# Rotary swap by on-chip transfers, and a turn of the identity ahead of rows of products

## What is computed

```
z = x @ w_in                       # u, v, q, k, val, gates side by side
q = rope(q.reshape(b, 256, 8 heads, 2, 64), cos, sin)
k = rope(k.reshape(b, 256, 8 heads, 2, 64), cos, sin)

def rope(x, cos, sin):             # the rotary embedding
    x1, x2 = split(x, 2, axis=-1)  # 32 values each
    return concatenate([x1 * cos - x2 * sin, x2 * cos + x1 * sin], axis=-1)

h_a = gelu(u) * sgu(layernorm(gelu(v)))   # "sgu": 128x128 products per group
o   = differential attention of q, k, val
m   = sigmoid(g1) * (h_a @ w_branch[0]) + sigmoid(g2) * (rmsnorm(o) @ w_branch[1])
out = m @ w_out
```

## Time and profile before

| | |
|---|---|
| median of 3 runs | 1830.66 us (1828.44 to 1833.03) |
| the profiled execution | 1825.48 us |
| its span in the profile | 1823.6 us |
| granted TensorE clock, mean | 0.995 |
| TensorE busy | 1789.7 us (98%) |
| DVE, ACT, POOL busy | 1136.4, 867.9, 247.0 us |
| DMA, mean | 181 GB/s, 53.2% of the 16 engines on SP's queue |

### The profile page before, as it was taken

The page is one execution under the profiler, slowest core; times in us unless marked ns, Lnnn a source line. Parts: engine busy times, 40 slices in busy tenths (PEclk is TensorE's granted clock), DMA queues, the critical chain, the costliest instruction groups (busy, mean ns, idle before and its releaser), DMA issues.

```text
span 1823.6 us, 31041 instructions
## 1 busy us (share of the span) xinstructions
PE 1789.7 (98%) x12819; PEld 1617.9 (89%) x12819; DVE 1136.4 (62%) x1735; ACT 867.9 (48%) x1412; POOL 247.0 (14%) x264
## 2 busy tenths in 40 slices
PE   9999999999999999999999999999999999999999
PEld 8998699999899879996899997999776877879999
DVE  5754587676766466655675876566655655565553
ACT  5454344664444435443535753545345355445543
POOL 2000232121200020001231212000111443100000
PEclk9999999999999999999999999999999999999999
DMA  8665654545666666754755455775443433346663
GB/s 285 195 219 192 233 186 159 165 139 191 206 208 209 204 208 231 231 185 161 250 169 185 135 168 193 234 242 182 165 152 93 110 98 93 117 159 190 203 194 111
DMA packets 252396, 330.56 MB, mean 181 GB/s; under 512 B 13162, under 2 KB 213072, under 8 KB 252256
## 3 DMA queue, kind: packets, MB, share of 16 engines
q1 hardware_dynamic: 248240, 315.31, 53.2%
q0 software_dynamic: 4016, 13.27, 2.1%
HBM read 327.51 MB, written 1.05 MB: 180 GB/s over the span
## 4 chain that ended last, share of the span: by engine, by line
PE 64%; issue 24%; DVE 6%; POOL 2%; ACT 2%; DMA 1%; POOLq 0%; DVEq 0%; ACTq 0%
PE bank L714 14%; PE bank L717 14%; PE bank L715 14%; PE bank L737 5%; PE bank L739 5%; PE bank L740 5%; DVE X L1930 1%; DVE wlo L1852 1%; ACT whi L1402 1%; PE bank L1250 1%; PE bank L1272 1%; POOL rs L2447 1%; DMA G<-in_lam_dram 1%; PE bank L898 1%; PE bank L936 1%
## 5 line engine op out<-in xcount | busy, mean ns | idle before, releaser
L1852 DVE TENSOR_TENSOR wlo<-raw,whi 128x1024 fp32r<-128x1024 f32 x537 | 663.8, 1241 | 374.6 <-ACT whi L1402 370.5
L1402 ACT ACTIVATE whi<-raw 128x1024 fp32r<-128x1024 f32 x549 | 574.4, 1052 | 393.6 <-PE bank L740 171.7
L714 PE MATMUL bank<-XTh,whi 128*128 128x256 f32 x1984 | 560.7, 283 | 0.0
L717 PE MATMUL bank<-XTh,wlo 128*128 128x256 f32 x1984 | 551.8, 278 | 2.9 <-DVE wlo L1852 2.9
L715 PE MATMUL bank<-XTl,whi 128*128 128x256 f32 x1984 | 551.6, 278 | 0.0
L717 PEld LDWEIGHTS bank<-XTh,wlo 128*128 128x128 f32 x1984 | 372.9, 188 | 3.3 <-DVE wlo L1852 3.3
L715 PEld LDWEIGHTS bank<-XTl,whi 128*128 128x128 f32 x1984 | 374.8, 189 | 1.0
L714 PEld LDWEIGHTS bank<-XTh,whi 128*128 128x128 f32 x1984 | 372.9, 188 | 2.9
L714 PE MATMUL bank<-HCh,whi 128*128 128x256 f32 (+1 forms) x880 | 252.5, 287 | 0.9 <-DVE tmp L2343 0.9
L717 PE MATMUL bank<-HCh,wlo 128*128 128x256 f32 (+1 forms) x880 | 248.1, 282 | 0.0
L715 PE MATMUL bank<-HCl,whi 128*128 128x256 f32 (+1 forms) x880 | 248.1, 282 | 0.0
(11 more groups left out here) (342 smaller groups left out, 2419.6 us busy)
## 6 DMA issues: line engine op xcount, KB each, us to landing
raw<-in_ffn_w_dram SPq DMA_DIRECT2D x131, 1024.0 KB, 5.1
raw<-in_w_in_dram SPq DMA_DIRECT2D x76, 1024.0 KB, 5.0
raw<-in_w_mod_dram SPq DMA_DIRECT2D x24, 1024.0 KB, 5.0
raw<-in_w_branch_dram SPq DMA_DIRECT2D x16, 1024.0 KB, 5.0
raw<-in_w_out_dram SPq DMA_DIRECT2D x12, 1024.0 KB, 4.9
raw<-in_w_ffn_gate_dram SPq DMA_DIRECT2D x11, 1024.0 KB, 5.1
raw<-in_w_ffn_up_dram SPq DMA_DIRECT2D x11, 1024.0 KB, 5.1
raw<-in_w_ffn_down_dram SPq DMA_DIRECT2D x8, 1024.0 KB, 5.1
```

The costliest lines, as they stand in the source:

```text
L714: e.matmul(o, hi[:, k, w0:w0 + nc_], xh, start=first and k == 0, stop=False)
L717: m = e.matmul(o, lo[:, k, w0:w0 + nc_], xh, start=False, stop=last and k == nk - 1)
L1402: e.activation(hi_part(n), raw_part(n), ACTF.Copy).then_inc(WHI.did(n), 1)
L1852: e.tensor_tensor(lo_part(n), raw_part(n), hi_part(n).bitcast(F32), ALU.subtract).then_inc(WLO.did(n), 1)
```

## The change

**Rotation.** `rotate` and `perm` leave TensorE. After its copy of qk n into `s`, ACT waits for that copy's own semaphore and starts four transfers of 32 partitions by 256 values (32 KB each) from `s` to `u`, each to the partitions of the other block; one of four new semaphores `ROT` counts them. DVE multiplies `s` with cos one round after the copy, and `u` with sin (in place, now from SBUF) two rounds after it. POOL adds two rounds after. The ring `mtmp` has six buffers, and `u` n needs the sum of n - 3 to be through. `settle` makes one transpose of the identity into an unused part of a bank: ahead of the 16 products qk, and at the end of `modulation`, of which it takes over the semaphore. The table of constants loses 128 columns. The pieces below are, in this order: TensorE (three), ACT (`turned` and its rounds), DVE, POOL.

```diff
+            def settle(b):
+                return e.transpose(bank[b][:, 256:384], ident, ident)
...
-                        mm = e.matmul(bank[b][:, 2 * j:2 * j + 2], SUMS[i][m][:, j * 128:(j + 1) * 128], sel[:, at:at + 2],
-                                      start=m == 0, stop=m == 1)
-                mm.then_inc(MOD.did(("columns", g)), 1)
+                        e.matmul(bank[b][:, 2 * j:2 * j + 2], SUMS[i][m][:, j * 128:(j + 1) * 128], sel[:, at:at + 2],
+                                 start=m == 0, stop=m == 1)
+                settle(b).then_inc(MOD.did(("columns", g)), 1)
...
-                def rotate(n):
-                    b = 4 + n % 2
-                    q.wait_ge(AMX, ("qk", l, n))
-                    empty(b)
-                    e.matmul(bank[b][:, 0:T], perm, mtmp[tm[l].slot["s", n]][:, :], start=True, stop=True).then_inc(
-                        SMALL.did(("perm", l, n)), 1)
-                    emptied[b] = ((DMX, ("sin", l, n)),)
+                empty(3)
+                settle(3)
                 for n in range(16):
...
                     emptied[b] = ((AMX, ("qk", l, n)),)
-                    if n:
-                        rotate(n - 1)
...
+                def turned(n):
+                    ring_free(q, tm[l], ("u", n))
+                    q.wait_ge(AMX, ("qk", l, n))
+                    for p in range(0, 128, 32):
+                        e.dma_start(mtmp[tm[l].slot["u", n]][p:p + 32, :], mtmp[tm[l].slot["s", n]][p ^ 32:(p ^ 32) + 32, :]).then_inc(
+                            ROT[n % 4].did(("turned", l, n), by=16), 16)
+
                 for n in range(16):
                     w.pass_by(1)
                     q.wait_ge(MM, ("qk", l, n))
                     ring_free(q, tm[l], ("s", n))
                     e.activation(mtmp[tm[l].slot["s", n]][:, :], bank[n % 4][:, 0:T], ACTF.Copy).then_inc(AMX.did(("qk", l, n)), 1)
+                    turned(n)
...
                 for n in range(16):
                     w.pass_by(1)
                     if n:
-                        rotate(n - 1)
+                        times_cos(n - 1)
+                    if n > 1:
+                        times_sin(n - 2)
+                times_cos(15)
...
                 for n in range(16):
                     w.pass_by(1)
-                    if n:
-                        rotate(n - 1)
+                    if n > 1:
+                        rotate(n - 2)
```

More of the change, by code:

```diff
@@ L32 @@
 C_ID, C_SHARED, C_CM = 0, 128, 128
-C_COS, C_SIN, C_PERM, C_FIRST = 384, 640, 896, 1024
+C_COS, C_SIN, C_FIRST = 384, 640, 896
 C_COSG, C_SING, C_PERMG, C_SCAN, C_GM, C_IN, C_NEG, C_CMB, C_ALL = (
-    1024, 1280, 1536, 1664, 2432, 2688, 2944, 3200, 3202)
+    896, 1152, 1408, 1536, 2304, 2560, 2816, 3072, 3074)
 R_GB, R_DG, R_C, R_CC, R_N1, R_N2, R_BM, R_BA, R_GN, R_NQ, R_NK, R_ALL = (
@@ L393, in program @@
         BIAS = [signal(f"s_bias{h}") for h in range(8)]
+        ROT = [signal(f"s_rotary{i}") for i in range(4)]
         MM, TURN, SMALL, MOD = [signal("s_pe_" + n) for n in ("gemm", "turn", "small", "mod")]
@@ L437, in program @@
         sb(xst, "gap1", [128, 68])
-        cm, cos, sin, perm = csa[:, 0:256], csa[:, 256:512], csa[:, 512:768], csa[:, 768:896]
+        cm, cos, sin = csa[:, 0:256], csa[:, 256:512], csa[:, 512:768]
         def ffn_bufs(st, name, at=STANDS):
@@ L453, in program @@
             G = sb(st, "G", [128, 16, T])
-            mtmp = some(st, "mtmp", 4, [128, T])
+            mtmp = some(st, "mtmp", 6, [128, T])
             sm = sb(st, "sm", [128, 16])
@@ L547, in program @@
         for l in range(2):
-            r = Ring(4)
+            r = Ring(6)
             for n in range(16):
-                r.use(("s", n), (SMALL, ("perm", l, n)), (DMX, ("cos", l, n)))
-                if n:
-                    r.use(("u", n - 1), (PMX, ("rot", l, n - 1)))
+                r.use(("s", n), (ROT[n % 4], ("turned", l, n)), (DMX, ("cos", l, n)))
+                r.use(("u", n), (PMX, ("rot", l, n)))
             for n in range(8):
                 r.use(("g", n), (XLO, ("ha", l, n)))
-                if n == 0:
-                    r.use(("u", 15), (PMX, ("rot", l, 15)))
             for n in range(8):
@@ L1956, in mixer, with times_cos, times_sin @@
                     e.scalar_tensor_tensor(V[:, t, :], V[:, t, :], rs[:, t, 1:2], gb[:, 1, :], ALU.mult, ALU.add).then_inc(DMX.did(("v", l, t)), 1)
[L1958 to L1963, removed]
+                def times_cos(n):
+                    dst, j, scale = (Q, K)[n // 8], n % 8, (0.125, 1.0)[n // 8]
+                    q.wait_ge(AMX, ("qk", l, n))
                     e.scalar_tensor_tensor(dst[:, j, :], mtmp[tm[l].slot["s", n]][:, :], scale, cos, ALU.mult, ALU.mult).then_inc(
                         DMX.did(("cos", l, n)), 1)
+                def times_sin(n):
+                    u, scale = mtmp[tm[l].slot["u", n]], (0.125, 1.0)[n // 8]
+                    q.wait_ge(ROT[n % 4], ("turned", l, n))
+                    e.scalar_tensor_tensor(u[:, :], u[:, :], scale, sin, ALU.mult, ALU.mult).then_inc(DMX.did(("sin", l, n)), 1)
                 for n in range(16):
@@ L1983, in mixer @@
                     w.pass_by(1)
-                    if n == 0:
-                        rotate(15)
-                    else:
+                    if n < 2:
+                        times_sin(14 + n)
+                    if n:
                         low("ha", HAl, HAh, n - 1, mtmp[tm[l].slot["g", n - 1]])
@@ L2470, in rotate @@
                     dst, j = (Q, K)[n // 8], n % 8
+                    q.wait_ge(DMX, ("sin", l, n))
                     q.wait_ge(DMX, ("cos", l, n))
@@ L2483, in mixer @@
                     e.tensor_tensor(s[:, :], s[:, :], SG[:, n, :], ALU.mult).then_inc(PMX.did(("a", l, n)), 1)
-                    if n == 0:
-                        rotate(15)
+                    if n < 2:
+                        rotate(14 + n)
                 w.pass_b(8, 2)
```

6 lines of the change are left out of this document (1 added, 5 removed).

## The result

| | before | changed |
|---|---|---|
| median | 1829.76 us (1828.44 to 1833.03) | 1850.85 us (1848.42 to 1857.08) |
| ratio, 95% interval | 1 | 1.0118 [1.0086, 1.0149] |
| profiled execution, its span | 1825.48, 1823.6 us | 1848.42, 1846.7 us |
| the interval in layer 1 from the first qk product to val | 79.4 us | 92.6 us |
| TensorE busy | 98% | 96% |

The change makes the kernel 1.2% slower; the forecast was 1814.6 us. The mixers of the two layers lose 13.2 and 13.0 us, and the turns after `modulation` win some of it back.

A forecast was written before the change was run, and what follows sets the result against it. TensorE, busy 98%, was taken to bound the kernel, with ACT slowest in the changed qk rounds. 1825.48 - 5.3 (turns) - 10.8 (both mixers) + 5.2 (profiled execution to median) gave 1814.6 us, range 1807 to 1834.

The forecast's parts named there:

- Part 1, the turn: After `modulation`, one turn at five seams brings 1344 products from 117.8 to 113.3 ns: net 5.3 us won.
- Rival B: The turn doesn't set the pace or sets it to 118 ns; loss of 0.6 us there, 1820.5 us; chance 0.13.
- Part 2, what leaves TensorE: In the mixer, rotation products and waits go; TensorE alone would reach val 8.6 us earlier a layer.
- I take 0.42 for a start: One transfer start on ACT takes 0.42 us, four 1.68, so ACT's qk round is 3.17 us.
- rival C: Starts on ACT cost as much as L652's: 1833.6 us at 0.64, 1850 at 0.8; chance of above 0.58: 0.20.
- The sum 1.49 + 4d for ACT's round: ACT's qk round is its other work, 1.49 us, plus four transfer starts of d us each.
- first sign of being wrong: The forecast is wrong if a transfer start takes over 0.47 us or under 0.37.
- In sgu and the u rounds ACT catches up, having no transfers there: After qk 15 ends at 280.1, sgu adds 3.8 us and u 21.8, val at 305.7: 5.4 us earlier a layer.
- Part 3, the cover: Landing is hidden twice over, POOL's later sums take 0.74 us, weight chunks lose little with DMA at 0.59.
- The stop at round 3 for POOL's sum 0: ACT's round 3 starts wait for POOL's sum, 1.65 us beside busy DVE, until 248.3; then 3.17 us a round.
- Sum: Profiled 1825.48 less 5.3 for turns and 10.8 for both mixers, plus 5.2 to the median: 1814.6 us.

The follow-up runs named there:

- swap_no_turn: The changed kernel without any turn (transpose of the identity), rotation by transfers kept: 1856.3 us, ratio 1.0153 to the kernel before.
- mod_turn: The kernel before with only one transpose of the identity after each group of two-column products in `modulation`: 1818.4 us, ratio 0.9952.
- best_no_turn: The changed kernel with two starts each on ACT and SP, sgu adds ahead of DVE's round 14, eight ring buffers, no turns: 1819.9 us, ratio 0.9947.
- no_transfers: The changed kernel without any transfer of the swap; the product with sin reads the copy of qk itself: 1805.3 us, ratio 0.9862.
- split_sg13: The changed kernel with two starts on ACT and two on SP, and DVE's sgu adds ahead of round 14: 1808.6 us, ratio 0.9898.
- eight_starts: The changed kernel with each transfer cut in two, eight starts of 16 KB a round on ACT: 1927.9 us, one execution.
- sg13: The changed kernel with DVE's eight sgu adds moved ahead of its weight part of round 14, four starts still on ACT: 1829.9 us, ratio 1.0010.
- two_starts: The changed kernel with two transfers of 64 KB on ACT instead of four, leaving out the swap of blocks of 32: 1816.8 us, ratio 0.9928.
- split_starts: The changed kernel with two of each swap's four transfers started by SP instead of ACT: 1824.3 us, ratio 0.9967.
- sg_early: The changed kernel with DVE's eight sgu adds in round 14, one weight part later than ahead of that round: 1834.8 us, ratio 1.0034.

## Why the prediction was wrong

**Part 1, the turn:** right. The five seams run at 113 ns. As a size, 5.3 us agrees with one pair of runs (5.5 to 6.4, changed and swap_no_turn) and lies below two (8.8 with mod_turn, about 13 with best_no_turn); what those have beyond it isn't explained. Rival B is refuted. The Trainium skill, "TensorE: Matmul & The Clock Gate", section "Back-to-back issue gap", gives one distance for a number of columns, and gives it for the isolated product; the traces don't agree with it for a stream of them: both paces stand in every trace here, and a turn moves products from one to the other.

**Part 2, what leaves TensorE:** right in sum, 8.6 us a layer foretold and 8.4 with no_transfers, with two sizes off that cancel. The first four rounds ran at 118 ns and not at 113, and so TensorE stood 1.03 us at qk 4 instead of 1.6. In layer 1 of split_sg13 they ran at 113, and it stood 1.43: the low part sets when qk 4 goes on.

**Part 3, "I take 0.42 for a start":** wrong size. It was 0.61 (2.44 for four). "SP's number there barely depends on size" held. The forecast took weight chunks (one start of 1 MB and then another) for the nearest rows; the rows of L652, which it put into rival C, were nearer. The sum 1.49 + 4d for ACT's round held: 3.93 by it with 0.61, 3.91 in the trace, and with 8d within 0.1 in eight_starts (6.37 and 6.46). A start over 0.47 was the forecast's own first sign of being wrong. The Trainium skill, "DMA: Bandwidth & Descriptors", section "Issuing engines are not separate DMA queues", calls the time to initiate a transfer usually small relative to the transfer. A single start agrees, 0.61 against a landing of 2.5 us, but with four of them they are the largest part of ACT's round.

**"In sgu and the u rounds ACT catches up, having no transfers there":** this step failed, and it is the larger part of the error. The forecast followed ACT's lag only to TensorE's next weight part. It didn't follow it to DVE, whose adds for sgu stand behind DVE's waits for ACT. With rival C's formula at d = 0.61, which has no such coupling, val begins at 248.3 + 12 x 3.93 + 2.44 + 2.1 + 13.6 = 313.6, for a qk start at 231.67. sg13, which takes away only that coupling, has its qk start at 230.04 and val at 312.1: by the formula 312.0. So close an agreement is in part luck: the starts of round 3 came at 245.85 in sg13, where the shifted formula has 246.67, and the twelve rounds behind took 3.99 us in the mean and not 3.93. The changed kernel has 324.5. So from 305.7 (forecast) to 324.5 are 7.9 us by the size of a start and about 10.9 by the missing step: 10.3 of it sgu itself, and of these 1.6 the clock after the wait. The stages say the same: qk ends at 288.4 instead of 280.1, and sgu takes 10.3 us more than the 3.8 foretold. Rival C had the size of a start, but at d = 0.61 it gives 1825.48 + 5.1 - 5.3 + 5.2 = 1830.5 us, 20 below the result: the same step was missing in it. That is about what sg13 measured without the coupling (1829.9, ratio 1.0010). C's 1850 us for d = 0.8 is near the result for another reason, as no start was that long in the mean.

**Part 3, the cover:** landing (2.5 us), POOL's sum (0.74) and DMA share (0.59) bind nothing, as foretold. The stop at round 3 for POOL's sum 0, from which the forecast counts, hardly came in the changed kernel (0.05 us in layer 1, about 0.4 in layer 2), as the sum took 0.73 us and not 1.65 and ACT was late already. It came, with 3.7 us, in the kernels with two starts on ACT.

**Sum.** The mixers were to win 10.8 us and lost 26.2. With the 5.3 of the turns that is +20.9 us; the medians differ by 21.1, the profiled executions by 22.9.

## What to carry to other kernels

A transfer start is an instruction of its engine with a price of its own, per start and not per byte: multiply it by the starts a round, add it to that engine's other work, and compare the sum with the round of the bounding engine before moving anything there, an engine that looks idle included. Where that engine then lags, go through every consumer of it to the end, not only to the next wait: the lag comes out where a short operation stands in order behind one that waits for the lagging engine, and here moving eight adds ahead by two rounds was worth about 20 us. Without that coupling the weight parts made ahead hid a lag of 7.6 us almost whole (sg13). A wait can be hidden behind another in the same way: the ring of six buffers hardly kept ACT while it had four starts a round, and kept it 3.7 us a layer once it had two.

## What was not expected of the hardware

- A start of a small transfer from SBUF to SBUF takes about 0.6 us on ACT and on SP alike (four on ACT 2.44, eight on SP 4.97), at 16, 32 and 64 KB (eight_starts, the changed kernel, two_starts); the first of a row of them takes 0.47 to 0.51 on ACT. Two of 32 KB on ACT take 1.41 when SP starts its own in step (split_starts), 0.51 + 0.86; the first two of four in the changed kernel take 0.51 and 0.61.
- After waits of 3.83, 5.63 and 8.72 us at sgu TensorE's next 16 small products show 3.78 us in the rows (sg_early, split_starts, the changed kernel; clock 0.50 in all three), and 2.05 after one of 0.60 (sg13, clock 1.00). In the second layer of sg_early they show 2.91 after 4.30.
- One transpose of the identity behind two-column products sets the products of 256 columns that follow to 113 ns instead of 118. What makes the two paces isn't known.
